# Opening stage of a two-block kernel on one core: modulation tiles loaded into places of their own, the token norm moved from GpSimd to VectorE, modulation on ScalarE

## The reference, cut to what matters

```python
m_l = (sc_lat @ w_ada[l] + b_ada[l])[:, None, :]      # sc_lat = silu(c)
m_c = sc_ctx @ w_ada[l] + b_ada[l]                    # sc_ctx = silu(c_ctx)
sh1, sc1, g1, sh2, sc2, g2 = jnp.split(m_l, 6, axis=-1)
hl = modulate(rmsnorm(lat, norm_g[l, 0]), sh1, sc1)   # and the same for the context, hc
q, zf_fwd, zf_bwd, v, g = jnp.split(h @ w_in, 5, axis=-1)
```

## Time and profile before

| what | value |
| --- | --- |
| median of 3 runs | 933.65 us (933.64 to 934.96) |
| the profiled execution | 934.58 us, its span 932.5 us |
| TensorE busy | 904.8 us (97%) |
| VectorE busy | 645.4 us (69%) |
| ScalarE busy | 507.8 us (54%) |
| GpSimd busy | 24.1 us (3%) |
| mean granted TensorE clock | 0.996 |

### The profile page before, as it was taken

The page is one execution under the profiler, slowest core; times in us unless marked ns, Lnnn a source line. Parts: engine busy times, 40 slices in busy tenths (PEclk is TensorE's granted clock), DMA queues, the critical chain, the costliest instruction groups (busy, mean ns, idle before and its releaser), DMA issues.

```text
span 932.5 us, 17009 instructions
## 1 busy us (share of the span) xinstructions
PE 904.8 (97%) x6294; PEld 822.6 (88%) x6294; DVE 645.4 (69%) x1036; ACT 507.8 (54%) x798; POOL 24.1 (3%) x22
## 2 busy tenths in 40 slices
PE   6799999999999999999999999999999999999997
PEld 2368888888899999999999898999999799999996
DVE  3969488888887777677677866774466766555555
ACT  6652466666664665555556655544464565444443
POOL 0720000000000000000000000000000000000000
PEclk9899999999999999999999999999999999999999
DMA  8469663433335265655655343344445446555551
GB/s 309 167 252 339 246 213 127 138 132 132 127 112 173 64 217 182 198 173 171 201 178 160 131 158 121 134 168 160 167 148 200 153 160 224 180 180 186 192 185 45
DMA packets 45437, 160.92 MB, mean 173 GB/s; under 512 B 5200, under 2 KB 6608, under 8 KB 45264
## 3 DMA queue, kind: packets, MB, share of 16 engines
q1 hardware_dynamic: 43632, 156.56, 49.3%
q10 hardware_dynamic: 1760, 3.74, 1.1%
HBM read 159.23 MB, written 1.05 MB: 172 GB/s over the span
## 4 chain that ended last, share of the span: by engine, by line
PE 92%; DVE 3%; POOL 2%; ACT 1%; DMA 1%; issue 1%; SPq 0%; DVEq 0%; ACTq 0%
PE bank L420 22%; PE bank L422 21%; PE bank L421 21%; PE bank L1125 4%; PE bank L486 4%; PE bank L488 4%; PE bank L487 4%; POOL tok L1515 1%; PE bank L1186 1%; PE bank L1139 1%; PE bank L1228 1%; PE bank L1224 1%; PE bank L1208 1%; PE bank L1158 1%; DMA tok<-in_tok 1%; DVE arena L650 1%
## 5 line engine op out<-in xcount | busy, mean ns | idle before, releaser
L414 DVE TENSOR_TENSOR w_lo<-raw,w_hi 128x1024 fp32r<-128x1024 f32 x260 | 317.0, 1233 | 154.2 <-ACT w_hi L407 153.9
L420 PE MATMUL bank<-h_hi,w_hi 128*128 128x256 f32 (+1 forms) x1248 | 373.2, 299 | 1.9 <-DVE h_lo L602 0.6
L422 PE MATMUL bank<-h_hi,w_lo 128*128 128x256 f32 (+1 forms) x1248 | 366.9, 294 | 0.0
L421 PE MATMUL bank<-h_lo,w_hi 128*128 128x256 f32 (+1 forms) x1248 | 365.5, 293 | 0.0
L407 ACT ACTIVATE w_hi<-raw 128x1024 fp32r<-128x1024 f32 x260 | 269.7, 1051 | 111.3 <-PE bank L422 74.2
L420 PEld LDWEIGHTS bank<-h_hi,w_hi 128*128 128x128 f32 x1248 | 234.8, 188 | 12.1 <-issue 3.6
L421 PEld LDWEIGHTS bank<-h_lo,w_hi 128*128 128x128 f32 x1248 | 236.2, 189 | 6.3
L422 PEld LDWEIGHTS bank<-h_hi,w_lo 128*128 128x128 f32 x1248 | 233.8, 187 | 5.8
L420 PE MATMUL bank<-y_hi,w_hi 128*128 128x256 f32 x304 | 86.8, 286 | 0.0
L422 PE MATMUL bank<-y_hi,w_lo 128*128 128x256 f32 x304 | 85.8, 282 | 0.0
L421 PE MATMUL bank<-y_lo,w_hi 128*128 128x256 f32 x304 | 85.4, 281 | 0.0
(11 more groups left out here) (250 smaller groups left out, 1119.6 us busy)
## 6 DMA issues: line engine op xcount, KB each, us to landing
raw<-in_stream SPq DMA_DIRECT2D x260, 512.0 KB, 3.5
arena<-in_ada SPq DMA_DIRECT2D x24, 512.0 KB, 5.6
xres<-in_ada SPq DMA_DIRECT2D x8, 512.0 KB, 3.3
tok<-in_tok SPq DMA_DIRECT2D x4, 512.0 KB, 9.1
con<-in_con ACTq DMA_DIRECT2D x1, 1472.0 KB, 9.5
xres<-in_tok ACTq DMA_DIRECT2D x1, 1024.0 KB, 8.7
out<-arena SPq DMA_DIRECT2D x4, 256.0 KB, 2.1
arena<-in_post_mix ACTq DMA_DIRECT2D x1, 512.0 KB, 4.2
```

The lines of the kernel that those rows point to most:

```text
L414: dve.tensor_tensor(w_lo[c.slot][:, :], raw[c.slot][:, :], w_hi[c.slot][:, :].bitcast(F32), ALU.subtract).then_inc(S("split_lo"), 1)
L420: pe.matmul(dst, hi_w, a_hi, start=start, stop=False, skip_group_check=True)
L421: pe.matmul(dst, hi_w, a_lo, start=False, stop=False, skip_group_check=True)
L422: return pe.matmul(dst, lo_w, a_hi, start=False, stop=stop, skip_group_check=True)
```

## The change

Twelve of the ada tiles (chunks 4 to 9 and 11 to 16) get places of their own in `arena` (columns 512 to 12799) and are loaded two at a time in six transfers, of which three are issued without any wait, then chunk 10 behind `split_lo` 3, then the other three; chunk 17 follows at once, chunk 18 behind `split_lo` 11. The `mod_rows` move from `arena` to `xres`. GpSimd's program is left out. VectorE multiplies the tokens by `rstd` (8 tiles, four of them before quarter 0, four after chunk 11) and, once ScalarE has modulated a tile in place, copies it to `h_hi` and subtracts to get `h_lo`. ScalarE forms `rstd` after chunk 3 instead of behind chunk 7. TensorE begins with 12 matmuls of 128x128 on zeros into bank 0 (`WARM`). Two memsets of `arena` move from the start to behind the values. Several pairs of semaphores are merged into one (`tok_log` into `tok_rstd`, `e_qd` and its four sisters into `exps`, `d1` and `d3` into `distances`, and so on), with the same waits in the same order. The diff, cut to its core:

```diff
+def staged(n):
+
+    return (n if n < V_FIRST else n - 1) - RING if RING <= n < EARLY and n != V_FIRST else None
...
-        assert used[0] <= 9728
-        used[0] = 10240
-        mod_rows = [part(512) for _ in range(4)]
+        mod_rows = [xres[:, q * 512:(q + 1) * 512] for q in range(4)]
+        used[0] = TC
+        ada_raw = [part(D) for _ in range(2 * KT - RING)]
...
+            n = c.least
+            if staged(n) is not None:
+                act.wait_ge(S(f"ada_in{staged(n) // 2}"), 16)
+            elif n < EARLY:
+                act.wait_ge(S(f"loaded{c.slot}"), 16 if n < RING else 32)
+            else:
+                act.wait_ge(S(f"loaded{c.slot}"), c.round * 16 + (16 - 16 * SKIPPED[c.slot]))
+            if n >= RING:
                 act.wait_ge(S("multiplied"), c.n - (RING - 1))
-            act.activation(w_hi[c.slot][:, :], raw[c.slot][:, :], ACT.Copy).then_inc(S("split_hi"), 1)
+            act.activation(w_hi[c.slot][:, :], source(c), ACT.Copy).then_inc(S("split_hi"), 1)
+
+        def source(c):
+
+            return raw[c.slot][:, :] if staged(c.least) is None else ada_raw[staged(c.least)]
...
-            with sp.Fori(1, ADA_FIRST // RING) as i:
-                load_stream(i)
-
-
-            def load_one(n):
-                sp.wait_ge(S("split_lo"), n - RING + 1)
+
+            def load_ada(pair):
+                first = ada_number(RING + 2 * pair) * P
+                sp.dma_start(arena[:, TC + 2 * pair * D:TC + 2 * (pair + 1) * D].rearrange("p (c n) -> p c n", c=2),
+                             stream_in[first:first + 2 * P, :].rearrange("(c p) n -> p c n", p=P)).then_inc(S(f"ada_in{pair}"), 16)
+
+            def load_one(n, split):
+                sp.wait_ge(S("split_lo"), split)
                 load(stream_in, n * P, n % RING)
+
+            for pair in range(3):
+                load_ada(pair)
+            load_one(V_FIRST, 3)
+            for pair in range(3, KT - RING // 2):
+                load_ada(pair)
...
-            for n in range(ADA_FIRST, ADA_FIRST + 2 * AHEAD):
-                load_one(n)
+            for n, split in ((EARLY, 2), (EARLY + 1, V_FIRST + 1), (EARLY + 2, 4)):
+                load_one(n, split)
             load_mods(0)
             load_mods(1)
-            for n in range(ADA_FIRST + 2 * AHEAD, ADA_FIRST + KT + AHEAD):
-                load_one(n)
+            for n in range(EARLY + 3, ADA_FIRST + KT + AHEAD):
+                load_one(n, V_FIRST + 1 if n == EARLY + 3 else n - RING + 1)
...
-                    act.activation(h_hi[:, at:at + T], tok[:, at:at + T], ACT.Identity, scale=gain[:, k:k + 1],
-                                   bias=shift[:, k:k + 1]).then_inc(S("h_hi"), 1)
-
-
-            for n in range(KT):
+                    x = tok[:, at:at + T]
+                    act.activation(x, x, ACT.Identity, scale=gain[:, k:k + 1], bias=shift[:, k:k + 1]).then_inc(S("modulated"), 1)
+
+            for n in range(6):
                 hi(act, Chunk(n))
                 if n < 4:
                     x = slice(n * 2 * TC, (n + 1) * 2 * TC)
                     act.wait_ge(S(f"tok_in{n}"), 16)
                     act.activation(wide[:, x], tok[:, x], ACT.Square).then_inc(S("tok_squares"), 1)
-                if n == 5:
-                    act.wait_ge(S("lb_diff"), 1)
-                    act.activation(lb_d, lb_d, ACT.Exp).then_inc(S("lb_exp"), 1)
-                    copy_rows(0)
-                if n == 7:
+                if n == 3:
                     act.wait_ge(S("tok_summed"), 1)
                     act.wait_ge(S("eps"), 1)
-                    act.activation(rstd, psum[1][:, :], ACT.Ln, scale=1.0 / D, bias=eps).then_inc(S("tok_log"), 1)
-                    act.wait_ge(S("tok_log"), 1)
+                    act.activation(rstd, psum[1][:, :], ACT.Ln, scale=1.0 / D, bias=eps).then_inc(S("tok_rstd"), 1)
+                    act.wait_ge(S("tok_rstd"), 1)
                     act.activation(rstd, rstd, ACT.Exp, scale=-0.5).then_inc(S("tok_rstd"), 1)
+            copy_rows(0)
+            hi(act, Chunk(6))
+            hi(act, Chunk(7))
+            act.wait_ge(S("lb_diff"), 1)
+            act.activation(lb_d, lb_d, ACT.Exp).then_inc(S("lb_exp"), 1)
             hi(act, Chunk(KT))
             copy_rows(1)
             hi(act, Chunk(KT + 1))
-
             modulate(0)
             hi(act, Chunk(V_FIRST))
             modulate(1)
             hi(act, Chunk(V_FIRST + 1))
             modulate(2)
+            hi(act, Chunk(V_FIRST + 2))
             modulate(3)
-            for n in range(V_FIRST + 2, EARLY):
+            for n in range(V_FIRST + 3, EARLY):
                 hi(act, Chunk(n))
             copy_rows(2)
             hi(act, Chunk(EARLY))
+            copy_rows(3)
+            modulate(4)
             hi(act, Chunk(EARLY + 1))
-            copy_rows(3)
-
-            for k in range(4, KT):
-                modulate(k)
-                if k == 5:
-                    hi(act, Chunk(EARLY + AHEAD))
+            modulate(5)
+            hi(act, Chunk(EARLY + 2))
+            modulate(6)
+            modulate(7)
...
+            pe.wait_ge(S("eps"), 1)
+            for _ in range(WARM):
+                pe.matmul(psum[0][:, 0:P], xres[:, 0:P], xres[:, 0:P], start=True, stop=True, skip_group_check=True)
...
-        @block.gpsimd
-        def _(pool):
-
...
+            dve.memset(xres[:, 0:P], 0.0)
             dve.memset(eps, EPS).then_inc(S("eps"), 1)
-            dve.memset(sc_T, 0.0)
-            dve.memset(k_e[0], 0.0)
...
+            def norm_tokens(k):
+
+                if k == 0:
+                    dve.wait_ge(S("tok_rstd"), 2)
+                x = tok[:, k * TC:(k + 1) * TC]
+                dve.tensor_tensor(x, x, rstd, ALU.mult).then_inc(S("tok_normed"), 1)
+
+            def split_tokens(k):
+
                 x = slice(k * TC, (k + 1) * TC)
+                dve.wait_ge(S("modulated"), 2 * k + 2)
+                dve.tensor_copy(h_hi[:, x], tok[:, x]).then_inc(S("h_hi"), 2)
+                dve.wait_ge(S("h_hi"), 2 * k + 2)
                 dve.tensor_tensor(h_lo[:, x], tok[:, x], h_hi[:, x].bitcast(F32), ALU.subtract).then_inc(S("h_lo"), 2)
 
+            for n in range(4):
                 lo(dve, Chunk(n))
+            dve.wait_ge(S("par_in"), 16)
+            dve.tensor_tensor(lb_m, p1("lb0", 0, 16), p1("lb1", 0, 16), ALU.max).then_inc(S("lb_step"), 1)
+            dve.wait_ge(S("lb_step"), 1)
+            dve.tensor_tensor(lb_d[:, 0:16], p1("lb0", 0, 16), lb_m, ALU.subtract)
+            dve.tensor_tensor(lb_d[:, 16:32], p1("lb1", 0, 16), lb_m, ALU.subtract).then_inc(S("lb_diff"), 1)
+            norm_tokens(0)
+            norm_tokens(1)
+            lo(dve, Chunk(4))
+            norm_tokens(2)
+            lo(dve, Chunk(5))
+            norm_tokens(3)
             quarter(0)
+            lo(dve, Chunk(6))
+            lo(dve, Chunk(7))
             lo(dve, Chunk(KT))
             quarter(1)
             lo(dve, Chunk(KT + 1))
+            split_tokens(0)
             lo(dve, Chunk(V_FIRST))
+            split_tokens(1)
             lo(dve, Chunk(V_FIRST + 1))
+            for k in range(4, KT):
+                norm_tokens(k)
+            split_tokens(2)
+            lo(dve, Chunk(V_FIRST + 2))
+            split_tokens(3)
+            for n in range(V_FIRST + 3, EARLY):
                 lo(dve, Chunk(n))
+            quarter(2)
             lo(dve, Chunk(EARLY))
+            quarter(3)
+            split_tokens(4)
             lo(dve, Chunk(EARLY + 1))
+            split_tokens(5)
+            lo(dve, Chunk(EARLY + 2))
+            split_tokens(6)
+            split_tokens(7)
...
+            dve.memset(sc_T, 0.0)
+            dve.memset(k_e[0], 0.0)
...
+                                   scale=-1.0, bias=b_buf[:, total:total + 1]).then_inc(S("exps"), 1)
+                act.wait_ge(S("distances"), h * 4 + 2)
+                act.activation(e_qe, d1, ACT.Exp).then_inc(S("exps"), 1)
```

More of the change, by code:

```diff
@@ L413, in lo @@
             dve.wait_ge(S("split_hi"), c.n + 1)
-            dve.tensor_tensor(w_lo[c.slot][:, :], raw[c.slot][:, :], w_hi[c.slot][:, :].bitcast(F32),
+            dve.tensor_tensor(w_lo[c.slot][:, :], source(c), w_hi[c.slot][:, :].bitcast(F32),
                               ALU.subtract).then_inc(S("split_lo"), 1)
@@ L842, in out_rstd @@
                 act.wait_ge(S("o_summed"), h + 1)
-                act.activation(o_rs, total, ACT.Ln, scale=1.0 / P, bias=eps).then_inc(S("o_log"), 1)
-                act.wait_ge(S("o_log"), h + 1)
+                act.activation(o_rs, total, ACT.Ln, scale=1.0 / P, bias=eps).then_inc(S("o_rstd"), 1)
+                act.wait_ge(S("o_rstd"), h * 2 + 1)
                 act.activation(o_rs, o_rs, ACT.Exp, scale=-0.5).then_inc(S("o_rstd"), 1)
@@ L1506, in _ @@
                        [grown(t % 4) for t in (JM - 2, JM - 1)], False, True)
-        @block.gpsimd
-        def _(pool):
-            pool.wait_ge(S("tok_rstd"), 1)
-            def norm_tokens(k):
```

(59 more changed lines are left out.)

60 lines of the change are left out of this document (23 added, 37 removed).

## The result

The changed kernel takes 938.85 us (median of 6 runs, 937.33 to 939.46); the kernel before took 934.27 us (median of 6, 933.64 to 936.43) beside it. The ratio is 1.0037, 95% interval 1.0025 to 1.0049: slower by 3.5 us as the ratio has it, 2.3 to 4.6 us. The profiled execution took 938.64 us, its span 936.9, the mean granted clock 0.987, against 934.58, 932.5 and 0.996.

What follows compares the result with a forecast made beforehand. TensorE, busy 97% of the span, was taken to bound the kernel, keeping opening delays to the end. values(1) 3.0 us later plus 0.95 to values(2) made +4.0 on 933.65: 937.6, range 932.8 to 940.8.

Steps and rivals of the forecast that it cites:

- From rstd to the values: VectorE's queue from its first scaling to the start of values(1): 55.7 us against 52.66, 3.0 us later.
- The last sum: TensorE's last sum of squares, which rstd waits for: taken to end at 23.31 us.
- The 1.4 us from sum to first scaling: From the start of Ln to the first reader of rstd: 1.4 us, putting VectorE's first scaling at 24.75.
- The work of 27.3 us: VectorE's scalings (4.9), 14 lo (16.0), four token splits (4.6) and quarters 0 to 2 (1.85) before values(1).
- Each copy: VectorE's copy in a token split: taken as 0.48 us, with 0.42 by the Trainium skill's figures.
- The waits of 3.5: VectorE's waits for TensorE before quarters 0, 1 and 2: together 2.6 to 5.3 us, taken as 3.5.
- From values(1) to values(2): Stretch with lo of chunk 18 now behind the split: 7.35 us against 6.4, 0.95 later.
- What costs nothing: GpSimd's leaving, later modulation tiles, moved memsets, the opening filler before TensorE's first work, and merged semaphores add no time.
- B: Rival: filler gives full clock when the sums begin at 10.42; sum ends 20.5, +1.2 us, 934.9; chance 0.27.
- C: Rival: only arrival and GpSimd bound, VectorE runs its queue through from rstd to chunk 17; -2.3 us, 931.3; chance 0.13.
- the hole at `rstd`: VectorE idle while waiting for rstd, about 6 us from 18 to 24.7 us.

Runs made afterwards that it cites:

- gpsimd_scales: Changed kernel with GpSimd, not VectorE, multiplying the eight token tiles by rstd: 940.96 us, ratio 1.0058 to the kernel before.
- filled_holes: Changed kernel with further idle 128x128 matmuls in TensorE's holes behind the last sum, behind the first turn and before values(0): 937.12 us, ratio 1.0022 to the kernel before.
- chunk18_early: Changed kernel with hi and lo of chunk 18 put back in front of row copy 3 and quarter 3: 938.01 us, ratio 1.0031 to the kernel before.
- clock_from_start: Changed kernel with 14 opening matmuls instead of 12 and 10 dummy matmuls behind ada tile 0: 937.00 us, ratio 1.0017 to the kernel before.
- all_moved_clock: Changed kernel with the edits of rstd_late, chunk18_early and clock_from_start, four scalings moved before quarter 3, and dummy matmuls behind ada 6 and before values(0): 928.51 us.
- rstd_late: Changed kernel with rstd formed behind hi of chunk 6, and lo of chunks 4 to 6 and quarter 0 before VectorE's first scaling: 932.21 us, ratio 0.9973.

## Why the prediction was right

I forecast 937.6 in 932.8 to 940.8 and slower with 0.62; the changed kernel is slower, at 938.85. Of the +4.0 us forecast, +3.5 came by the ratio, +4.6 by the medians and +4.3 at the start of `values(2)` in the two profiles. The mechanism held, a stall for `rstd` followed by VectorE's queue with waits for TensorE. The closeness of the figure is in part luck: it came out of two errors that nearly cancelled, and the steps show them.

**From rstd to the values.** The last sum was taken from the kernel before, at 23.31; it ended at 22.15. That is when the clock rose, and most likely not the change's doing: the changed kernel's opening, untouched, gave 12.69 us behind the first square in its own profile and 13.98 in that of gpsimd_scales. Of the kernel before there is one profile, with 14.00. The 1.4 us from sum to first scaling were 1.41. The work of 27.3 us was right to 0.1: 55.88 - 23.56 = 32.3 us, less the waits of 1.87, 2.66 and 0.38, leave 27.4 with the hand-over. Each copy took 0.42 or 0.43, below the 0.49 to 0.68 between which the prediction had put it; the estimate from the Trainium skill's figures (VectorE: DVE Perf Modes, the perf-mode tier table) was 0.42, and the trace agrees. It saved nothing, since the subtract starts 0.10 us behind the copy's end and not 0.05: a split still took 1.14 (40.90 to 42.04). The waits of 3.5 were 4.91, the term that was mis-sized: both waits came at their half-clock ends (2.0 and 2.9), because the clock stayed low through the whole of both. filled_holes shows the other end: with the clock held, the three waits are 0.92, 1.13 and 0.39, 2.4 together, where the prediction had 2.6 at full clock. -1.16 and +1.41 gave 55.88 against 55.7.

**From values(1) to values(2).** 7.35 forecast, 7.52 measured. chunk18_early, with 6.49, shows that the 1.0 us is chunk 18's new place, as the step had it.

**What costs nothing.** The opening matmuls ended ahead of ada tile 0, the idle time ahead of head 0 is 12.26 us, no engine waits for a transfer between 24 and 60 us, and from `values(2)` on nothing changed by more than 0.1 us. All of it as forecast.

**The rivals.** B (full clock from 10.42 through the filler) did not happen in the changed kernel's profile: TensorE stood idle for 2.04 us ahead of the first sum, which ran at half clock. (The `lo` of chunk 3 that the prediction gives to ScalarE there is VectorE's.) The mechanism exists all the same; with the gap filled (clock_from_start) the sums end 20.58, where B had 20.5. Its profile then starts `values(2)` 2.3 us later than before, where B had 1.2 for it, since B too kept the later waits at their middle value. The granted clock was full for ada tile 0 in every kernel with the filler. It was still full at the first sum both times that the gap was filled (to within 0.55 us in all_moved_clock), and with the opening filler alone in one profile of seven. The Trainium skill's rule (TensorE: Matmul & The Clock Gate, Part 1), by which activity releases the throttled clock, agrees with the trace to that extent. C needed VectorE to run its queue through; it waited for 4.91 us before `values(1)`, and 5.33 ahead of them.

**What I had not seen.** The prediction listed the hole at `rstd` and the waits before quarters as separate terms. rstd_late shows that they hang together: with three chunks ahead of the wait, hole and waits shrink in one edit, by 6.5 us. And the loads bring 0.8 to 1.7 us by themselves, which the new order uses up.

## What to carry to other kernels

In a queue written out by hand, a wait belongs behind all the work that does not need it: the same instructions took 3.5 us more or 2.5 us less than the kernel before, by whether `rstd` was asked for ahead of three chunks or after them. When work moves onto an engine, look for a wait of that engine to put it in, here quarter 3's 3.49 us, before paying for it on the path. And where single executions scatter by a microsecond, cut the timeline at two or three events that the edits don't touch, and compare the pieces.

## What was not expected of the hardware

The length of the opening varies from one profile to the next by two things that no edit explains (but for the two kernels with work in front of the first sum). ScalarE's first square started between 9.17 and 10.61 us, when its tokens had landed, with the same loads issued ahead of it. And the last sum ended 11.4, 12.4 to 12.7, 13.4 or 14.0 us behind that, by when the granted clock rose; twice at 14.0 and once at 11.4 without an edit to show for it. Here are the first squares of the kernel before and of gpsimd_scales:

```profile
9.31 1.06 ACT L763 ACTIVATE wide<-tok 128x1024 f32<-128x1024 f32 x1 [3.09 <-DMA tok<-in_tok]
```
```profile
10.45 1.06 ACT L786 ACTIVATE wide<-tok 128x1024 f32<-128x1024 f32 x1 [4.61 <-DMA tok<-in_tok]
```

So the sums ended anywhere from 21.1 to 24.4 us in the profiles of kernels without work in front of the first sum, and 24 runs of the kernel before spread over 4.2 us (933.03 to 937.21). With work in front of it the second part stayed put, at 11.41 in both kernels that had it.
